# Row sums for the norms and the softmax as four 32-column tiles behind the rope matmuls, and another order of the first loads, in an 8-core hybrid attention block

## The chip, the cores and the metric

The kernel runs on the 8 cores of one Trainium2 chip. Each core computes one half of the positions of one of four batch entries (1024 of 2048), all heads, with no exchange between cores. The metric is the device time of the slowest core, in microseconds (us). Engines are named as in the profile: PE is TensorE (PEld its weight loads), ACT is ScalarE, DVE is VectorE, POOL is GpSimd, SP is SyncE, which only starts transfers here.

## What is computed

The reference, cut to what the change touches:

```python
h = rmsnorm(x, norm_g); z = h @ w_in            # split into latents, rope key, gates, conv inputs
q  = rmsnorm(q_a, q_lat_g) @ w_uq               # 16 heads x (128 + 64 rope)
kv = rmsnorm(kv_a, kv_lat_g) @ w_ukv            # 16 heads x (128 key + 128 value)
k  = concat(k_nope, k_pe for every head)
q, k = rmsnorm(q, q_norm_g), rmsnorm(k, k_norm_g)     # over the 192 columns of a head
q, k = rope on the last 64 columns
attn = softmax(q @ k.T * 192**-0.5) @ v               # all 2048 keys
y_attn = (attn * silu(gate_a)) @ w_branch_attn        # beside it a gated 3-tap convolution branch
x = x + merge(y_attn, y_conv) @ w_out                 # then a gated per-layer embedding is added
```

Activations lie with channels on partitions and positions in columns, so the sum of squares of a head's query or key, and the sum of a softmax, run over partitions. The kernel makes them on PE, with a matrix of ones as one operand.

## The kernel before

**Stages.** Opening: 16 tiles of x (513 KB each, six buffers) and 16 pieces of the latent weights (w_lq, w_lk; eight staging buffers) come in on SP's queue in a written order `seq`; ACT scales each x tile, DVE casts each weight piece, PE multiplies (`q_lat`, then `kv_own`). Then gate tiles and the other half's keys, to 240 us. From there the head loop runs to about 905 us; after it come the merge, the output projection and the embedding gate.

**The head loop.** For each head there are 16 key steps (kt 0 to 15, 128 keys each). In step kt the program emits for PE: `emit_nope` of the next step (two 512-column matmuls: scores), in odd steps `emit_rope` of the next two steps (four matmuls of 64 rows, which run two at a time), and `emit_PV` of this step (two 512-column matmuls). For ACT it emits `emit_exp` of the next step (128x1024). Score banks are 0 to 3, in two pairs by the step's parity.

Between these, one `quantum` of the convolution branch runs in each step (four matmuls of 512 columns, or five or six of 342). Where a quantum ends its PSUM bank (`ends_bank()`), it is emitted ahead of the scores (`early`), elsewhere behind them. The pattern repeats every two heads. In even heads the early steps are kt 2, 5, 8, 11 and 14, in odd heads kt 0, 4, 8, 12 and 15.

**Pieces.** During head h the queries, keys and values of head h+1 are made, in `up_pieces`: `kup` (keys, two matmuls; ACT copies the bank, then squares it), `qrope`, `qnope` (four matmuls; copy and square), `vup` (values; one copy), and the sums `qss` (query, three matmuls of 512 columns with `onesL`, `onesR`, `onesB`) and `kss` (key, 16 matmuls with one column each). `lsum` (softmax of the head before, fp32) is at kt 1. All pieces use one PSUM bank, bank 7 (`bU`): a piece can't begin until the one before it has been read out. `widen` spreads the factors of a sum over the partitions by four transfers on SP.

Engines take their instructions in the order in which the program emits them; an instruction that must wait holds those behind it. The pieces stand first in a step:

```python
fn, after = pieces.get(kt, (None, None))
if fn:
    fn(bU)
if kt == 1 and lsum:
    lsum(bU)
...
early = ends_bank()
```

Of the kernel before, what the change touches and what calls it, by code (L numbers as in the profile page):

```python
# [167 lines left out]
def build_nc():  # L168
# [12 lines left out]
    wlq_d = din("w_lq", [8, 128, 1024])  # L181
    wlk_d = din("w_lk", [8, 128, 768])
# [6 lines left out]
    with ExitStack() as es:  # L189
# [44 lines left out]
        onesL = small(BF16, 128, "onesL")  # L234
        onesR = small(BF16, 128, "onesR")
# [75 lines left out]
        def cast():
# [47 lines left out]
        for b_, boxes in ((onesL, ((0, 128, 0),)), (onesR, ((0, 128, 64),)), (onesB, ((0, 64, 0), (64, 128, 64)))):
            P.op("dve", lambda h, b_=b_: h.memset(b_.ap, 0.0), writes=[b_])  # L360
            for r0, r1, c0 in boxes:
                P.op("dve", lambda h, b_=b_, r0=r0, r1=r1, c0=c0: h.memset(b_.ap[r0:r1, c0:c0 + 64], 1.0), reads=[b_], writes=[b_])
# [645 lines left out]
        for h in range(NH):  # L1008
# [275 lines left out]
```

How the kernel before makes its waits and increments, by code:

```python
    def emit(self, eng, h, sems):  # L146
        waited = {}
        for o in self.ops[eng]:
            need = {}
            for d in o.deps:
                if d.slot is not None:
                    k, v, s = id(d.slot), d.val, d.slot.sem
                else:
                    if d.eng == "pe" and eng == "pe":
                        continue
                    k, v, s = d.eng, d.count, sems[d.eng]
                if waited.get(k, 0) < v and need.get(k, (0, None))[0] < v:
                    need[k] = (v, s)
            for k, (v, s) in need.items():
                h.wait_ge(s, v)
                waited[k] = v
            inst = o.fn(h)
            if o.slot is not None:
                inst.then_inc(o.slot.sem, 16)
            elif o.signal:
                inst.then_inc(sems[eng], 1)
```

## Time and profile before

| What | Value |
|---|---|
| Median of 3 runs | 1532.65 us (1531.38 to 1534.86) |
| The profiled execution | 1532.65 us, of which the span of core 6 is 1531.1 us |
| Spans of the 8 cores | 1523.3 to 1531.1 us |
| PE busy | 1496.2 us (98% of the span), 7854 matmuls |
| DVE, ACT, POOL busy | 839.5 us, 711.6 us, 224.0 us |
| Granted PE clock, mean by core | 0.997 to 1.000 |

The rows are of core 6, the slowest. A matmul's row has its start and a modelled duration, which holds some 0.16 us of pipeline behind the last column. Matmuls follow each other more closely than that, so the distance of two starts tells the cost, and a short wait of PE does not show as idle.

### The profile page before, as it was taken

The page shows a single profiled execution, that of the slowest core. Times are in us where ns is not written, and L with a number is a line of the kernel's source. Part 1 is how long each engine was busy: PE and PEld are TensorE (multiplying, and loading weights), DVE is VectorE, ACT ScalarE, POOL GpSimd, SP SyncE. Part 2 cuts the span into 40 slices and gives each one's busy share as a digit, 9 for nine tenths or more (in the row PEclk, how much of TensorE's full clock was granted, in tenths as well). Part 3 has the DMA queues.
Part 4 walks back from the last instruction along what each step waited for, and adds up shares of the span by engine and source line. Part 5 has one row for each costly group of instructions (what it writes and reads, how often), then busy time and mean ns, then how long its engine had stood idle before and what let it go on. Part 6 is the DMA issues. An engine that isn't in the chain of part 4 may idle for free.

```text
span 1531.1 us, 22610 instructions; the slowest of 8 cores (1523.3 to 1531.1 us)
## 1 busy us (share of the span) xinstructions
PE 1496.2 (98%) x7854; PEld 673.6 (44%) x7854; DVE 839.5 (55%) x1043; ACT 711.6 (46%) x966; POOL 224.0 (15%) x245
## 2 busy tenths in 40 slices
PE   6899999999999999999999999999999999999998
PEld 2344444444444444444444444444444444444443
DVE  5566565777766776766677762222222222444555
ACT  5565678777777777777776641100011100112111
POOL 0000000221303131222223121000010001000000
PEclk9999999999999999999999999999999999999999
DMA  8937542333333222333333217354453536984641
GB/s 271 265 71 178 122 83 58 72 57 72 72 71 60 54 59 58 72 70 72 69 59 63 56 35 124 56 90 70 75 91 55 97 60 139 219 174 76 135 117 73
DMA packets 52071, 144.15 MB, mean 94 GB/s; under 512 B 7668, under 2 KB 7670, under 8 KB 51832
## 3 DMA queue, kind: packets, MB, share of 16 engines
q0 software_dynamic: 23328, 78.13, 30.3%
q1 hardware_dynamic: 28480, 64.52, 14.3%
q8 instruction: 65, 1.06, 0.3%
q14 instruction: 46, 0.38, 0.1%
q10 hardware_dynamic: 152, 0.05, 0.0%
HBM read 188.81 MB, written 8.39 MB: 129 GB/s over the span
## 4 chain that ended last, share of the span: by engine, by line
PE 88%; DVE 3%; ACT 3%; issue 3%; DMA 2%; SPq 0%; DVEq 0%; ACTq 0%
PE ps L257 86%; PE ps L256 2%; DMA xo_89<-x_own 1%; DMA xo_88<-x_own 1%; DVE acc L271 1%; ACT eb_172 L260 0%; SPq L251 0%; ACT eb_173 L260 0%; ACT P_208 L260 0%; ACT P_210 L260 0%; ACT fall L260 0%; ACT P_209 L260 0%; DVE yb L263 0%; DVE Qn_204 L263 0%; ACT sqs_140 L260 0%
## 5 line engine op out<-in xcount | busy, mean ns | idle before, releaser
L271 DVE TENSOR_TENSOR acc<-acc,P_210 128x1024 f32<-128x1024 f32 x75 | 99.3, 1324 | 13.2 <-ACT P_210 L260 10.3
L271 DVE TENSOR_TENSOR acc<-acc,P_208 128x1024 f32<-128x1024 f32 x75 | 97.8, 1304 | 14.8 <-ACT P_208 L260 11.7
L271 DVE TENSOR_TENSOR acc<-acc,P_209 128x1024 f32<-128x1024 f32 x74 | 98.9, 1337 | 11.6 <-ACT P_209 L260 8.8
L257 PE MATMUL ps<-Qn_204,Kn_200 128*128 128x512 bf16 x256 | 76.6, 381 | 0.0
L257 PE MATMUL ps<-Qn_205,Kn_201 128*128 128x512 bf16 x256 | 76.2, 379 | 0.0
L260 ACT ACTIVATE mt_258<-mt_258 128x512 f32<-128x512 f32 x16 | 10.1, 632 | 123.6 <-DVE mt_258 L271 123.6
L260 ACT ACTIVATE mt_257<-mt_257 128x512 f32<-128x512 f32 x16 | 10.1, 632 | 120.0 <-DVE mt_257 L271 120.0
L251 POOL DMA_DIRECT2D ring_126<-w_tiles x23 | 12.9, 561 | 347.7 <-PE ps L257 283.6
L260 ACT ACTIVATE P_210<-ps,sk_54 128x1024 bf16<-128x1024 f32 x43 | 47.9, 1114 | 13.9 <-PE ps L257 7.4
L260 ACT ACTIVATE P_209<-ps,sk_55 128x1024 bf16<-128x1024 f32 x43 | 48.0, 1117 | 11.6 <-PE ps L257 10.8
L260 ACT ACTIVATE P_208<-ps,sk_54 128x1024 bf16<-128x1024 f32 x43 | 47.9, 1115 | 11.7 <-PE ps L257 7.2
L260 ACT ACTIVATE P_208<-ps,sk_55 128x1024 bf16<-128x1024 f32 x43 | 48.0, 1116 | 10.4 <-PE ps L257 9.8
L260 ACT ACTIVATE P_210<-ps,sk_55 128x1024 bf16<-128x1024 f32 x42 | 47.0, 1118 | 10.5 <-PE ps L257 8.0
L260 ACT ACTIVATE P_209<-ps,sk_54 128x1024 bf16<-128x1024 f32 x42 | 46.8, 1114 | 10.1 <-PE ps L257 5.5
L257 PE MATMUL ps<-Qr_206,KrT 64*128 64x512 bf16 x256 | 40.8, 385 | 1.9 <-ACT P_208 L260 0.7
L257 PE MATMUL ps<-Qr_207,KrT 64*128 64x512 bf16 x256 | 39.4, 381 | 0.8 <-ACT P_209 L260 0.3
L263 DVE SCALAR_TENSOR_TENSOR mt_262<-mt_258,ps 128x512 f32<-128x512 f32 x16 | 11.0, 688 | 44.0 <-PE ps L257 44.0
L274 POOL TENSOR_TENSOR zb<-zb,rst 128x512 f32<-128x512 f32 x16 | 31.8, 1990 | 22.2 <-ACT ebc L260 22.2
L271 DVE TENSOR_TENSOR mt_260<-ps,rst 128x512 f32<-128x512 f32 x16 | 11.1, 692 | 43.5 <-PE ps L257 43.5
L260 ACT ACTIVATE tp_308<-tp_306 128x512 f32<-128x512 f32 x16 | 10.1, 632 | 53.0 <-DVE tp_306 L271 53.0
L257 PEld LDWEIGHTS ps<-Qn_205,Kn_201 128*128 128x128 bf16 x256 | 22.4, 97 | 27.2 <-issue 9.4
L263 DVE SCALAR_TENSOR_TENSOR mt_261<-mt_257,ps 128x512 f32<-128x512 f32 x16 | 11.0, 688 | 41.8 <-PE ps L257 41.8
(1428 smaller groups left out, 4074.9 us busy)
## 6 DMA issues: line engine op xcount, KB each, us to landing
fb<-f_218 SPq DMA_DIRECT2D x128, 128.0 KB, 2.4
ring_127<-w_tiles POOLq DMA_DIRECT2D x28, 512.0 KB, 6.8
ring_129<-w_tiles POOLq DMA_DIRECT2D x28, 512.0 KB, 5.8
ring_126<-w_tiles POOLq DMA_DIRECT2D x23, 512.0 KB, 5.7
ring_128<-w_tiles POOLq DMA_DIRECT2D x22, 512.0 KB, 6.6
ringm_266<-w_tiles POOLq DMA_DIRECT2D x14, 512.0 KB, 6.3
ringm_265<-w_tiles POOLq DMA_DIRECT2D x9, 512.0 KB, 7.1
t_223<-q_221 SPq DMA_DIRECT2D x64, 64.0 KB, 2.0
```

What stands on the lines that cost most here:

```text
L251: return P.dma(eng, lambda h: h.dma_start(out=o_ap, in_=in_ap), slot, reads=reads, writes=[b], deps=deps)
L256: return P.op("pe", lambda h: h.matmul(bank_ap, lhsT=lhsT, rhs=rhs, start=start, stop=stop, skip_group_check=True), reads=reads, writes=wr ...
L257: return P.op("pe", lambda h: h.matmul(bank_ap, lhsT=lhsT, rhs=rhs, start=start, stop=stop), reads=reads, writes=writes)
L260: return P.op("act", lambda h: h.activation(out=out, in_=in_, func=func, **kw), reads=reads, writes=writes)
L263: return P.op("dve", lambda h: h.scalar_tensor_tensor(out=out, in0=in0, scalar=scalar, in1=in1, op0=op0, op1=op1), reads=reads, writes=writes)
L271: return P.op("dve", lambda h: h.tensor_tensor(out=out, in0=in0, in1=in1, op=op), reads=reads, writes=writes)
L274: return P.op("pool", lambda h: h.tensor_tensor(out=out, in0=in0, in1=in1, op=op), reads=reads, writes=writes)
```

## The change

It has three parts.

1. **The sums.** `qss` becomes eight matmuls, each 32 columns of the array wide with 256 moving columns; `kss` becomes four of 32 by 512, then a transpose on DVE; `lsum` becomes four of 32 by 256. Each of the four tiles writes another 32 partitions of bank 7. The two ACT instructions behind `qss` and `lsum` shrink from 512 to 256 columns. `widen` makes the same bytes in four transfers, each source row read four times. The query factors are applied in three places (kt 10, 12, 13) in place of one.
2. **The order in a step.** The pieces are emitted behind scores, exp and rope. `kup` 1 moves from kt 6 to kt 2, `qrope` from 2 to 3, `qnope` from 4 and 5 to 5 and 6.
3. **The opening.** Three small loads (positions, `sel`, `cols`) go ahead of all else on SP in place of ACT's queue; w0 is requested before x0; there are four staging buffers in place of eight; w_lq and w_lk lie in another layout, each load still 4 KB or 3 KB per partition.

```diff
-        stage = [at((RING0 if i < 4 else W0 + 45408) + i % 4 * 4096, F32, 1024, f"stage{i}") for i in range(8)]
+        stage = [at(W0 + 45408 + i * 4096, F32, 1024, f"stage{i}") for i in range(4)]
...
-        seq = ("x0 w0 x1 w1 x2 x3 w2 x4 x5 w3 x6 x7 w4 x8 x9 w5 x10 x11 w6 w7 x12 w8 w9 x13 w10 w11 x14 w12 w13 x15 w14 w15").split()
+        seq = ("w0 x0 x1 w1 x2 x3 w2 x4 x5 w3 x6 x7 w4 x8 x9 w5 x10 x11 w6 w7 x12 w8 w9 x13 w10 w11 x14 w12 w13 x15 w14 w15").split()
...
-                    if int(n[1:]) - 8 >= cast_n[0]:
+                    if int(n[1:]) - 4 >= cast_n[0]:
...
+        ld("sp", posi, pos_d, out_ap=posi.ap[0:2, :])
+        ld("sp", sel, sel_d, out_ap=sel.ap[0:2, :])
+        ld("sp", cols, cols_d)
         issue()
-        ld("act", posi, pos_d, out_ap=posi.ap[0:2, :])
-        ld("act", sel, sel_d, out_ap=sel.ap[0:2, :])
-        ld("act", cols, cols_d)
...
+        def quarters(q):
+
+            return q // 2, slice((q % 2) * 256, (q % 2) * 256 + 256), slice(q * 32, q * 32 + 32)
+
         def widen(src):
 
-            for qb in range(2):
-                for r in range(2):
-                    ld("sp", fb, src.ap[qb * 64:qb * 64 + 64, :], out_ap=fb.ap[r * 64:r * 64 + 64, qb * 512:(qb + 1) * 512], reads=[src])
+            (pitch, _), (_, n) = src.ap.ap
+            for q in range(4):
+                rows = bass.AP(src.ap.tensor, src.ap.offset + q * 32 * pitch, [[pitch, 32], [0, 4], [1, n]])
+                ld("sp", fb, rows, out_ap=fb.ap[:, q * n:(q + 1) * n], reads=[src])
...
             def qss(bk):
-                for i, l_ in enumerate((onesL, onesR, onesB)):
-                    mm(bk.ap, l_.ap, qsq[i].ap, i == 0, i == 2, [l_, qsq[i]], [bk])
-                act(f2.ap, bk.ap, AF.Ln, [bk, cols], [f2], bias=col(C_EPS), scale=1.0 / 192)
+                for part in range(2):
+                    for q in range(4):
+                        hf, n, r = quarters(q)
+                        l_ = onesB.ap[:, hf * 64:hf * 64 + 32] if part else ones.ap[:, 0:32]
+                        s_ = qsq[2] if part else qsq[hf]
+                        mm(bk.ap[r, 0:256], l_, s_.ap[:, n], part == 0, part == 1, [onesB, ones, s_], [bk], skip=True)
+                act(f2.ap, bk.ap[:, 0:256], AF.Ln, [bk, cols], [f2], bias=col(C_EPS), scale=1.0 / 192)
...
             def kss(bk):
-                for j in range(16):
-                    s_ = ksq[j // 4]
-                    mm(bk.ap[:, j:j + 1], s_.ap[:, (j % 4) * 128:(j % 4 + 1) * 128], ones.ap[:, 0:1], j == 0, j == 15, [s_, ones], [bk], skip=True)
-                tt(skt[p].ap, bk.ap[:, 0:16], sspe.ap, ADD, [bk, sspe], [skt[p]])
+                kv_ = ksqa.ap.rearrange("p (t q n) -> p q t n", q=4, n=32)
+                for q in range(4):
+                    mm(bk.ap[q * 32:q * 32 + 32, :], ones.ap[:, 0:32], kv_[:, q], True, True, [*ksq, ones], [bk], skip=True)
+                tr = t12[1]
+                P.op("dve", lambda h: h.transpose(out=tr.ap, in_=bk.ap), reads=[bk], writes=[tr])
+                tt(skt[p].ap, tr.ap[:, 0:512:32], sspe.ap, ADD, [tr, sspe], [skt[p]])
...
-            return {0: (pc(kup, 0), None), 2: (pc(qrope), qrope_out), 4: (pc(qnope, 0), None), 5: (pc(qnope, 1), lambda bk: rot()), 6: (pc(kup, 1), None), 7: (pc(qss), None),
-                    8: (pc(kup, 2), None), 9: (pc(kup, 3), None), 10: (pc(vup, 0), lambda bk: qfin()), 11: (pc(kss), None), 12: (pc(vup, 1), None), 13: (pc(vup, 2), None),
-                    14: (pc(vup, 3), None)}
+            return {0: (pc(kup, 0), None), 2: (pc(kup, 1), None), 3: (pc(qrope), qrope_out), 5: (pc(qnope, 0), None), 6: (pc(qnope, 1), lambda bk: rot()), 7: (pc(qss), None),
+                    8: (pc(kup, 2), None), 9: (pc(kup, 3), None), 10: (pc(vup, 0), lambda bk: qn_out(0)), 11: (pc(kss), None), 12: (pc(vup, 1), lambda bk: qn_out(1)),
+                    13: (pc(vup, 2), lambda bk: qr_out()), 14: (pc(vup, 3), None)}
...
             def lsum(bk):
-                for qb in range(2):
-                    r = slice(qb * 64, qb * 64 + 64)
-                    mm(bk.ap[r, :], onesf.ap[:, r], acc.ap[:, qb * 512:(qb + 1) * 512], True, True, [onesf, acc], [bk], twin=qb == 1)
-                act(f2.ap, bk.ap, AF.Ln, [bk], [f2], scale=2.0)
+                for q in range(4):
+                    mm(bk.ap[q * 32:q * 32 + 32, 0:256], onesf.ap[:, 0:32], acc.ap[:, q * 256:(q + 1) * 256], True, True, [onesf, acc], [bk], skip=True)
+                act(f2.ap, bk.ap[:, 0:256], AF.Ln, [bk], [f2], scale=2.0)
...
-                if fn:
-                    fn(bU)
-                if kt == 1 and lsum:
-                    lsum(bU)
                 if kt == 15:
...
                     emit_exp(g + 1)
                     if first:
                         emit_rope(g + 2, True)
+                if fn:
+                    fn(bU)
+                if kt == 1 and lsum:
+                    lsum(bU)
```

**PE's order in steps kt 8 and 9 of an odd head.** Step 8 is an early one. `kvaT` rows are a `kup` piece, `xh` rows the convolution quantum, `Qn` rows the scores, `Qr` rows rope, `P` rows PV. Before:

```order
L257 MATMUL ps<-kvaT_145,wup_187 128x512 [waits s_act]
L257 MATMUL ps<-kvaT_146,wup_187 128x512
L257 MATMUL ps<-xh_68,ring_129 128x512
L257 MATMUL ps<-xh_69,ring_129 128x512
L257 MATMUL ps<-xh_70,ring_129 128x512
L257 MATMUL ps<-xh_71,ring_129 128x512
L257 MATMUL ps<-Qn_205,Kn_201 128x512 x2
L257 MATMUL ps<-P_208,V_203 128x512 [waits s_act]
L257 MATMUL ps<-P_208,V_203 128x512
L257 MATMUL ps<-kvaT_145,wup_187 128x512 [waits s_act]
L257 MATMUL ps<-kvaT_146,wup_187 128x512
L257 MATMUL ps<-Qn_205,Kn_201 128x512 x2
```

The same place in the change, from the last matmul of the quantum:

```order
L255 MATMUL ps<-xh_69,ring_123 128x512
L255 MATMUL ps<-Qn_199,Kn_195 128x512 x2
L255 MATMUL ps<-kvaT_139,wup_181 128x512 [waits s_act]
L255 MATMUL ps<-kvaT_140,wup_181 128x512
L255 MATMUL ps<-P_202,V_197 128x512 x2
L255 MATMUL ps<-Qn_199,Kn_195 128x512 x2
L255 MATMUL ps<-Qr_201,KrT 128x512 x2
L255 MATMUL ps<-Qr_201,KrT 128x512 [waits s_act]
L255 MATMUL ps<-Qr_201,KrT 128x512
L255 MATMUL ps<-kvaT_139,wup_181 128x512 [waits s_act]
L255 MATMUL ps<-kvaT_140,wup_181 128x512
```

Between the two pieces there stood the quantum, one pair of scores and PV. Now there stand PV, one pair of scores and a block of rope.

**PE's order around the query sum, kt 7 of an odd head.** `qsq` rows are `qss`. Before:

```order
L257 MATMUL ps<-P_209,V_203 128x512
L257 MATMUL ps<-qsq_215,onesL 128x512 [waits s_act]
L257 MATMUL ps<-qsq_216,onesR 128x512
L257 MATMUL ps<-qsq_217,onesB 128x512
L257 MATMUL ps<-Qn_205,Kn_201 128x512 x2
L257 MATMUL ps<-Qr_207,KrT 128x512 x2
```

Now:

```order
L255 MATMUL ps<-Qn_199,Kn_195 128x512 x2
L255 MATMUL ps<-Qr_201,KrT 128x512 x2
L255 MATMUL ps<-Qr_201,KrT 128x512 [waits s_act]
L255 MATMUL ps<-Qr_201,KrT 128x512
L254 MATMUL ps<-qsq_206,ones 32x256 [waits s_act]
L254 MATMUL ps<-qsq_206,ones 32x256
L254 MATMUL ps<-qsq_207,ones 32x256 x2
L254 MATMUL ps<-qsq_208,onesB 32x256 x4
```

The three full matmuls ahead of the scores have become eight small ones directly behind rope.

## Rows read from the trace of the kernel before

**Rows 1.** Windows: window, length, busy us (and instructions) of each engine, clock, DMA.
```profile
0.00:50.00 50.00, 31.04 (x103) 11.03 (x103) 28.48 (x44) 31.08 (x33) 0.20 (x4) 0.97 0.85 277
240.00:905.00 665.00, 661.39 (x4015) 297.72 (x4014) 469.87 (x513) 476.92 (x649) 159.14 (x123) 1.00 0.31 62
```

**Rows 2.** Timeline of PE: softmax sum, scores, rope; start, duration, instruction.
```profile
449.70 1.08 PE L257 MATMUL ps<-acc,onesf 128*64 128x512 f32 x4
450.71 0.61 PE L257 MATMUL ps<-Qn_205,Kn_201 128*128 128x512 bf16 x2
451.25 0.60 PE L257 MATMUL ps<-Qr_207,KrT 64*128 64x512 bf16 x4
451.78 0.39 PE L257 MATMUL ps<-xh_56,ring_128 128*128 128x512 bf16 x1
```

**Rows 3.** Timeline of PE: `qrope`, `qss` and `kss`, with what follows them.
```profile
453.18 0.41 PE L257 MATMUL ps<-qaT_72,wup_187 128*64 128x512 bf16 x2
453.42 0.38 PE L257 MATMUL ps<-qaT_73,wup_187 128*64 128x512 bf16 x2
...
466.26 0.38 PE L257 MATMUL ps<-qsq_215,onesL 128*128 128x512 bf16 x1
...
466.91 0.59 PE L257 MATMUL ps<-Qn_205,Kn_201 128*128 128x512 bf16 x2
...
476.41 0.24 PE L256 MATMUL ps<-ones,ksq_211 128*128 128x1 bf16 x4
...
476.81 0.59 PE L257 MATMUL ps<-Qn_205,Kn_201 128*128 128x512 bf16 x2
```

**Rows 4.** Timeline, kt 8 to 9 of an odd head; brackets: idle time, releaser.
```profile
470.57 0.59 PE L257 MATMUL ps<-Qn_205,Kn_201 128*128 128x512 bf16 x2
...
471.32 1.11 ACT L260 ACTIVATE P_210<-ps,sk_55 128x1024 bf16<-128x1024 f32 x1 [0.27 <-PE ps L257]
...
472.33 0.58 ACT L918 CAST Kn_200<-ps 128x512 bf16<-128x512 f32 x1
...
472.80 0.61 ACT L260 ACTIVATE ksq_214<-ps 128x512 bf16<-128x512 f32 x1
```

**Rows 5.** Timeline, kt 2 to 3 of an even head.
```profile
413.77 0.59 PE L257 MATMUL ps<-Qn_204,Kn_200 128*128 128x512 bf16 x2
...
414.52 1.11 ACT L260 ACTIVATE P_209<-ps,sk_54 128x1024 bf16<-128x1024 f32 x1 [0.86 <-PE ps L257]
...
415.17 0.39 PE L257 MATMUL ps<-Qr_206,KrT 64*128 64x512 bf16 x2
...
415.78 0.39 PE L257 MATMUL ps<-Qr_206,KrT 64*128 64x512 bf16 x2 [0.23 <-ACT P_209 L260]
```

**Rows 6.** Timeline, kt 11 to 12 of an odd head.
```profile
478.75 0.59 PE L257 MATMUL ps<-P_209,V_203 128*128 128x512 bf16 x2
479.17 0.17 DVE L271 TENSOR_TENSOR skt_52<-ps,sspe 128x16 f32<-128x16 f32 x1
...
479.48 0.22 PE L256 MATMUL ps<-wup_187,kvaT_145 128*128 128x128 bf16 x1
```

**Rows 7.** The costliest groups: instruction, count | busy us, mean ns | idle before.
```profile
L271 DVE TENSOR_TENSOR mt_260<-ps,rst 128x512 f32<-128x512 f32 x16 | 11.1, 692 | 43.5 <-PE ps L257 43.5
```

**Rows 8.** Timeline: SP's four transfers of one `widen`, and their first user.
```profile
468.86 2.43 SPq L251 DMA_DIRECT2D fb<-f_218  x4
...
477.66 0.73 DVE L263 SCALAR_TENSOR_TENSOR Qn_204<-q_220,colx,fb 128x512 bf16<-128x512 f32 x1
```

**Rows 9.** Timeline of the opening (SPq and ACTq are transfer requests).
```profile
1.07 0.54 ACTq L251 DMA_DIRECT2D posi<-pos_row  x1
...
1.91 0.37 ACTq L251 DMA_DIRECT2D cols<-cols  x1
...
11.36 1.15 ACT L260 ACTIVATE xh_56<-xo_84,cols 128x1026 bf16<-128x1026 f32 x1 [7.49 <-DMA cols<-cols]
...
44.36 1.15 ACT L260 ACTIVATE xh_67<-xo_89,cols 128x1026 bf16<-128x1026 f32 x1 [1.61 <-DMA xo_89<-x_own]
...
48.52 0.38 PE L257 MATMUL ps<-xh_56,wlk_116 128*128 128x512 bf16 x1 [0.97 <-ACT qraw_82 L421]
```

More of the change, by code:

```diff
@@ L180, in build_nc @@
     sel_d = din("sel", [2, 128])
-    wlq_d = din("w_lq", [8, 128, 1024])
-    wlk_d = din("w_lk", [8, 128, 768])
+    wlq_d = din("w_lq", [128, 16, 512])
+    wlk_d = din("w_lk", [128, 16, 384])
     wup_d = din("w_up", [NH, 128, 1280])
@@ L233, in build_nc @@
         onesf = small(F32, 128, "onesf")
-        onesL = small(BF16, 128, "onesL")
-        onesR = small(BF16, 128, "onesR")
         onesB = small(BF16, 128, "onesB")
@@ L304, in ld_part @@
             kind, i = order[n]
-            b = stage[n % 8]
+            b = stage[n % 4]
             if kind == "q":
-                ld("sp", b, wlq_d[i])
+                ld("sp", b, wlq_d[:, i * 2:(i + 1) * 2, :], out_ap=b.ap.rearrange("p (c n) -> p c n", c=2))
             else:
-                ld("sp", b, wlk_d[i], out_ap=b.ap[:, 0:768])
+                ld("sp", b, wlk_d[:, i * 2:(i + 1) * 2, :], out_ap=b.ap[:, 0:768].rearrange("p (c n) -> p c n", c=2))
         def cast():
@@ L314, in cast @@
             kind, i = order[n]
-            b = stage[n % 8]
+            b = stage[n % 4]
             if kind == "q":
@@ L349, in casts_to @@
                     issue()
+        ld("sp", posi, pos_d, out_ap=posi.ap[0:2, :])
+        ld("sp", sel, sel_d, out_ap=sel.ap[0:2, :])
+        ld("sp", cols, cols_d)
         issue()
-        ld("act", posi, pos_d, out_ap=posi.ap[0:2, :])
-        ld("act", sel, sel_d, out_ap=sel.ap[0:2, :])
-        ld("act", cols, cols_d)
         P.op("dve", lambda h: h.memset(ones.ap, 1.0), writes=[ones])
-        act(sspe.ap[:, 0:1], ones.ap[:, 0:1], AF.Copy, [ones], [sspe])
         P.op("dve", lambda h: h.memset(onesf.ap, 1.0), writes=[onesf])
[L359 to L362, printed above, removed]
+        P.op("dve", lambda h: h.memset(onesB.ap, 0.0), writes=[onesB])
+        for r in (0, 64):
+            P.op("dve", lambda h, r=r: h.memset(onesB.ap[r:r + 64, r:r + 64], 1.0), reads=[onesB], writes=[onesB])
         vcopy(posf.ap[0:2, :], posi.ap[0:2, :], [posi], [posf])
@@ L397, in q_lat @@
                 mm(banks[i].ap, w_.ap[:, o + m * 128:o + (m + 1) * 128], xh[kc].ap[:, qb * 512:(qb + 1) * 512], kc == first, kc == last, [w_, xh[kc]], [banks[i]])
+        act(colx.ap[:, 3:4], ones.ap[:, 0:1], AF.Copy, [ones], [colx])
+        casts_to("x0")
         kv_next = 0
@@ L837, in build_nc @@
         Pt = [take(BF16, T, f"P{i}") for i in range(3)]
-        ksq = [take(BF16, 512, f"ksq{i}") for i in range(4)]
+        ksqa = take(BF16, S, "ksqa")
+        ksq = [Buf(ksqa.ap[:, i * 512:(i + 1) * 512], f"ksq{i}") for i in range(4)]
+        for b in ksq:
+            b.alias = ksqa.alias
         qsq = [take(BF16, 512, f"qsq{i}") for i in range(3)]
-        f2 = take(F32, 512, "f2")
+        f2 = take(F32, 256, "f2")
         fb = take(F32, T, "fb")
@@ L1200, in part @@
         return np.ascontiguousarray(w.reshape(k // 128, 128, n).transpose(1, 0, 2))
-    def pairs(w):
-        k, n = w.shape
-        return np.ascontiguousarray(w.reshape(k // 256, 2, 128, n).transpose(0, 2, 1, 3).reshape(k // 256, 128, 2 * n))
     conv = np.stack([tiles(w_in[:, c:c + 1024]) for c in (C_CC, C_CX, C_GC, C_CB)], axis=1).reshape(32, 128, 2048)
@@ L1246, in _host_inputs @@
         "sel": ((np.arange(128) // 32 % 2)[None, :] == np.arange(2)[:, None]).astype(f32),
-        "w_lq": pairs(w_in[:, 0:512]),
-        "w_lk": pairs(np.concatenate([w_in[:, 512:768], kpe, kpe[:, perm]], axis=1)),
+        "w_lq": part(w_in[:, 0:512]),
+        "w_lk": part(np.concatenate([w_in[:, 512:768], kpe, kpe[:, perm]], axis=1)),
         "w_up": np.ascontiguousarray(wup),
```

13 lines of the change are left out of this document (6 added, 7 removed).

## The prediction

> **What bounds the kernel now.** I read the windows first. From 240 to 905 us, the head loop in which the change lies, PE is busy 661 of 665 us at the full clock, while DVE has 470 and ACT 477 [rows 1]. So a column taken from PE there is time, and so is each wait added to it; work added to DVE or ACT costs nothing until PE waits for it. Then I read PE's timeline, by the distance of starts. Three matmuls of 512 columns take 0.65 us [rows 3], so one is 0.217 and a pair 0.43. The scores at 450.71 should be through at 451.14, but rope starts at 451.25; rope's four matmuls, two at a time, should be through at 451.68, and the next full matmul starts at 451.78 [rows 2]. Each change between the full array and a tiled one thus costs 0.10 to 0.11 us, and a block of rope 0.11 + 0.43 + 0.10 = 0.64. Last I looked for places where PE waits. There are two kinds, and both matter below.
>
> The first kind stands after an early step that has no piece behind its scores. The scores start at 413.77, the exp on them at 414.52, and it ends at 415.63. The second half of rope, which overwrites the bank that this exp reads, was ready 0.22 behind 415.17, at 415.39, and starts at 415.78, 0.15 after the exp's end: PE lost 0.39 [rows 5]. This stands once in each of the eight even heads 0 to 14. The second kind is at `vup` in the seven odd heads 1 to 13: PV should be through at 479.18, DVE frees bank 7 at 479.34, `vup` starts at 479.48, 0.30 late [rows 6].
>
> **What the sums save on PE.** `qrope` shows two tiles of 64 columns at once: a pair of them is 0.22 to 0.24, like one full matmul [rows 3]. I take it that four tiles of 32 do the same.
> - `qss`: 0.65 [rows 3] becomes two rounds of 256 columns, 0.22. It also lies between two tiled shapes, and no row shows whether PE pays for going from one to the other: 0 or 0.11. I take the nearest row, 0.10 [rows 2]. Saved: 0.33.
> - `kss`: 16 matmuls take 0.40 [rows 3]; one round of 512 columns and the 0.10 take 0.32. Saved: 0.08.
> - `lsum`: 1.01 from its start to the scores, 0.16 of it beyond its column time of 0.85 [rows 2], and 0.10 ahead of it: 1.11. Now half the columns, 0.43, and the 0.16: 0.59. Saved: 0.52.
> - `qrope` behind rope spares one change of shape: 0.10.
>
> That is 1.03 us a head, 15.5 for the 15 heads with pieces. Outside the loop the first head's `qss` gives 0.23 and the last `lsum` 0.43. In all 16.2 us.
>
> On tile-to-tile changes the Trainium skill (TensorEngine Tiling (Array Packing), Key Properties) says that changing the tiling mode, and not only the tile, drains the engine; no run here shows that step yet. By it the 0.10 above would stay.
>
> **What the order costs.** Bank 7 is one, and a piece waits until ACT has read the one before. Before, a piece stood first in its step, ACT read it at once, and the quantum, scores and PV lay between it and the next piece. Now ACT first gets the exp of the same step, since that is emitted ahead of the piece. Rows 4 give ACT's chain at just such a place: scores start at 470.57, exp at 471.32, copy at 472.33, square at 472.80, ending at 473.41; with the 0.15 of rows 5 the bank is free 2.99 us after the scores began [rows 4, 5]. In a step that is not early the quantum, up to four times 0.217 us, lies behind the piece as well, and this fits. In an early step the quantum lies ahead of the scores, so that PE comes to the next piece after scores 0.43, `kup` 0.43, PV 0.43, scores 0.43 and rope 0.64 = 2.36 us [rows 2, 3]. It waits 0.63.
> - Four places are of this kind: even heads kt 2 to `qrope` and kt 8 to `kup` 3; odd heads kt 0 to `lsum` and kt 8 to `kup` 3.
> - Even heads, `qnope` 0 (kt 5) to `qnope` 1: the exp, 0.32 (that is 0.75 less 0.43) behind its first pair of rope [rows 4], starts as `qnope` does; the copy waits for `qnope`'s end, 0.86 + 0.32 = 1.18, the square starts 0.47 later and ends at 2.26, the bank is free at 2.41. PE is back after 0.86 + 0.43 + 0.43 = 1.72. It waits 0.69.
> - Odd heads, kt 4 is early and has no piece any more: the wait of rows 5, 0.39.
> - `vup` 2 behind early `vup` 1 in odd heads: 0.75 + 1.01 + 0.58 + 0.15 = 2.49 against 2.37 (`vup` has eight matmuls of 128 columns where `kup` has two of 512), 0.12 [rows 4].
> - Even heads, `kss` (kt 11) to `vup` 1: bank 7 is freed by the transpose. No row shows one; the bounds are the 0.17 of a small DVE instruction [rows 6] and twice the 0.692 of one that reads 128x512 from PSUM [rows 7]. I take 0.69, the row nearest in shape. The sum's 0.22, the 0.32 to the next engine, 0.69 and 0.15 make 1.38 against 0.32 + 0.43 + 0.43 = 1.18, but part of the sum's drain lies under the wait: about 0.1 lost. With the lower bound nothing is lost, with the upper 0.7 more, 6 us over eight heads.
>
> Even heads lose 0.63 + 0.63 + 0.69 + 0.1 = 2.05, eight of them 16.4; odd heads 0.63 + 0.63 + 0.39 + 0.12 = 1.77, seven of them 12.4: 28.8 us. In return the waits of today go. In even heads `kup` now stands in kt 2 behind the scores and gives the exp 0.43 more: 8 x 0.39 = 3.1. In odd heads DVE has one query product ahead of `kss` in place of three, and PE comes later: 7 x 0.30 = 2.1 [rows 5, 6]. Together 5.2.
>
> **What costs nothing.** DVE gets the transpose and one product more, some 1.4 us a head, in a loop in which it is idle for 195 us [rows 1]; without that room it would cost 21 us. ACT's logarithms and exponentials on half the columns are off PE's path. The four transfers of `widen` have rows half as long; their requests end at 471.29 and the first user starts at 477.66 [rows 8], so even twice the request time, 2.43 us more, is hidden; if it were not, DVE would reach `kss` late, at the price of the upper bound above.
>
> **The opening.** Transfers are busy 0.85 of the first 50 us, at 277 GB/s [rows 1], and ACT waits for the twelfth x tile until 44.36, behind which PE's dense key matmuls start at 48.52 [rows 9]. The first big request is now made behind three small ones, whose requests take from 1.07 to 2.28 [rows 9]: 1.2 us later, and the same bytes stand ahead of the twelfth tile. So +1.2. From below: today the first tile waits for `cols` until 11.36 [rows 9], and the change has both by about 9 us (1 MB at 277 GB/s behind the requests); if the stream is not what holds, 2.4 us are gained. From above, four staging buffers for eight may leave the stream dry behind the casts; I allow as much again, +2.4. `xo_89` is ahead of all loads that wait so.
>
> **The sum** is made against the profiled execution, 1532.65 us with a span of 1531.1, which is also the median: 1532.65 - 16.2 - 5.2 + 28.8 + 1.2 = 1541.3, about 1541.
>
> **Rivals.**
> - *ACT is done in time* (faster). If the chain from scores to free bank fell from 2.99 below 2.36 us, the waits would vanish and the savings stay: 1541 less 28.8 is 1512. For it: ACT is idle a quarter of the loop. Against it: rows 5, where PE waits for the exp alone. Chance 0.12.
> - *Half of the waits.* PE's lost time in one place lets ACT and DVE run ahead, and later waits shrink: 1527 to 1535. Chance 0.13.
> - *The tiles do not run side by side.* Then qss takes 0.86, kss 0.86, lsum 1.71 of column time in place of 0.22, 0.22 and 0.43: 2.56 a head, 38 us, 1579. Rows 3 speak against it with two tiles. Chance 0.04.
> - *They run side by side, but start late.* If a round of four took a quarter longer than one tile, 0.22 a head, it would be 1544. The Trainium skill (TensorE: Matmul & The Clock Gate, Part 3) has three 32-column tiles at 2.38 times one; an estimate by that share is 0.23 a head, 1545. Chance 0.05.
> - *The transpose is twice the price*: 1547. Chance 0.06.
> - *The opening is not held by the stream*: 1541 - 1.2 - 2.4 = 1537. Chance 0.05.
>
> **How the numbers follow.** The forecast has 0.55. A measurement of this kernel can tell about 0.2%, 3 us: 1529.6 to 1535.7 is no change. Faster: the first rival and a third of the second, 0.16. The same: the rest of the second and the lower edge of the forecast, 0.09 + 0.07 = 0.16. Slower: 0.68. The range of 1527 to 1551 leaves out the first rival and the third, and a few hundredths at the edges; its ends are half the waits gone below, and the transpose's and the opening's upper bounds, 1541 + 6 + 1.2 with some late tiles, above. The forecast's own range is 1535 to 1547.
>
> **What would show it.** In the changed kernel's timeline `qss`, `kss` and `lsum` should take 0.2 to 0.6 us from their start to the next start, and lie directly behind rope. `qrope` and `kup` 3 of even heads and `lsum` and `kup` 3 of odd heads should start about 0.15 behind the end of ACT's square, some 0.6 late. An even and an odd head together should take 1.1 us more than now (3.82 of waits come, 0.69 go, 2.06 are saved). Wrong it would be if those pieces start without a gap, if rows of ACT show the copy ahead of the exp, or if PE's dense key matmuls start well before 48.

## The result and the profile after

| | Before | The change |
|---|---|---|
| Median | 1532.1 us | 1543.1 us |
| Ratio to before, 95% interval | | 1.0067 [1.0047, 1.0087] |
| Slowest span of the profiled execution | 1531.1 us (core 6) | 1541.8 us (core 1) |

Medians, here and in the table of the runs, are of the executions in which no half of the cores ran at a lowered clock; some expectations quote medians of all executions, up to 0.4 us higher.

The change is slower by 0.67%. The prediction had 1541, with slower as the likeliest sign. The loss is not made up as the prediction has it, though: the head loop is nearly as forecast, the opening has the other sign, and a loss of six to seven microseconds ahead of the loop was not seen.

First the window of the head loop in the changed kernel, with the columns of [rows 1]:

```profile
240.00:905.00 665.00, 641.25 (x3934) 292.02 (x3935) 487.18 (x540) 460.33 (x649) 147.10 (x119) 1.00 0.32 62
```

In the head loop PE is busy 641 us in place of 661. The columns are saved, but no time is gained: the 20 us are now idle, and the loop is longer. The timeline shows where. First two places where nothing waits: `lsum` in an even head, then `qss` and `kss`, each with the rope ahead and the row behind.

```profile
330.20 0.61 PE L255 MATMUL ps<-Qr_200,KrT 64*128 64x512 bf16 x4
...
330.74 0.64 PE L254 MATMUL ps<-acc,onesf 128*32 128x256 f32 x8
...
331.31 0.32 PE L255 MATMUL ps<-xh_59,ring_120 128*128 128x342 bf16 x1
...
346.91 0.61 PE L255 MATMUL ps<-Qr_200,KrT 64*128 64x512 bf16 x4
...
347.45 0.29 PE L254 MATMUL ps<-qsq_206,ones 128*32 128x256 bf16 x2
...
347.78 0.32 PE L255 MATMUL ps<-xh_59,ring_120 128*128 128x342 bf16 x1
...
358.37 0.40 PE L254 MATMUL ps<-ksqa,ones 128*32 128x512 bf16 x4
...
358.70 0.60 PE L255 MATMUL ps<-P_203,V_196 128*128 128x512 bf16 x2
358.89 0.72 DVE L936 STREAM_TRANSPOSE t_214<-ps 128x512 f32<-128x512 f32 x1 [0.80 <-PE ps L254]
```

From start to next start `lsum` takes 0.57, `qss` 0.33 and `kss` 0.33, where they took 1.01, 0.65 and 0.40 [rows 2, 3]. Four matmuls of 512 columns in 0.33, of which 0.22 is the time of one and 0.11 the change of shape: the four tiles run side by side. From rope's start to `lsum` there are 0.54, 0.43 of columns and 0.11: going from one tiled shape to another costs the same 0.11 as going to the full array does at these places.

Now step kt 8 to 9 of an even head, which answers to [rows 4], and `lsum` in an odd head:

```profile
349.83 0.59 PE L255 MATMUL ps<-Qn_198,Kn_194 128*128 128x512 bf16 x2
...
350.57 1.11 ACT L258 ACTIVATE P_204<-ps,sk_52 128x1024 bf16<-128x1024 f32 x1 [1.04 <-PE ps L255]
...
351.59 0.58 ACT L928 CAST Kn_195<-ps 128x512 bf16<-128x512 f32 x1
...
351.65 0.60 PE L255 MATMUL ps<-Qr_200,KrT 64*128 64x512 bf16 x4
...
352.05 0.61 ACT L258 ACTIVATE ksqa<-ps 128x512 bf16<-128x512 f32 x1
...
352.81 0.38 PE L255 MATMUL ps<-kvaT_139,wup_182 128*128 128x512 bf16 x1 [0.55 <-ACT ksqa L258]
...
371.96 0.60 PE L255 MATMUL ps<-Qr_201,KrT 64*128 64x512 bf16 x4
...
373.12 0.64 PE L254 MATMUL ps<-acc,onesf 128*32 128x256 f32 x8 [0.55 <-ACT ksqa L258]
```

Scores at 349.83, bank free for `kup` 3 at 352.81: 2.98 us. PE was ready at 351.65 + 0.43 + 0.10 = 352.18 and lost 0.63. `lsum` lost the same behind `kup` 0. The row names the square that PE waited for.

From the softmax sum in head 2 to that in head 14 there are six pairs of heads. They began at 324.90 and 826.93 before. Now the first is at 330.74 (above), and the last is

```profile
838.57 0.64 PE L254 MATMUL ps<-acc,onesf 128*32 128x256 f32 x8
```

A pair took 502.03 / 6 = 83.67 us and takes 507.83 / 6 = 84.64, 0.97 more. This measure serves for every run below.

Three rows of the slowest core of each profile divide the rest of the time: the sum of squares of x behind the opening, the first scores, the last softmax sum. Before:

```profile
70.31 1.03 PE L257 MATMUL ps<-accx,onesf 128*128 128x342 f32 x3
...
237.92 1.06 PE L257 MATMUL ps<-Qn_204,Kn_200 128*128 128x512 bf16 x2
...
904.40 1.08 PE L257 MATMUL ps<-acc,onesf 128*64 128x512 f32 x4
```

Now:

```profile
67.66 1.31 PE L255 MATMUL ps<-accx,onesf 128*128 128x342 f32 x4
...
241.37 1.06 PE L255 MATMUL ps<-Qn_198,Kn_194 128*128 128x512 bf16 x2
...
915.46 0.64 PE L254 MATMUL ps<-acc,onesf 128*32 128x256 f32 x8
```

The opening ends 2.65 us earlier, the stretch to the first scores is 6.1 longer (173.71 for 167.61), the loop 7.6 longer (674.09 for 666.48). With -0.4 behind the loop that is the 10.7 us between the spans. The 6.1 is in the first head's pieces, which are made ahead of the loop in the order of the same table:

```profile
219.94 2.40 SPq L249 DMA_DIRECT2D t_214<-q_212  x4
...
221.38 0.53 POOL L249 DMA_DIRECT2D ring_122<-w_tiles  x1 [9.20 <-PE ps L255]
...
226.95 0.59 ACT L884 COPY q_212<-ps 128x512 f32<-128x512 f32 x1 [3.16 <-DMA t_214<-q_212]
...
227.44 0.60 ACT L258 ACTIVATE qsq_207<-ps 128x512 bf16<-128x512 f32 x1
...
228.18 0.40 PE L254 MATMUL ps<-qsq_207,ones 128*32 128x256 bf16 x2 [4.11 <-ACT qsq_207 L258]
...
228.73 0.61 PE L255 MATMUL ps<-xh_64,ring_123 128*128 128x512 bf16 x1
...
233.40 0.57 PE L255 MATMUL ps<-xh_57,ring_123 128*128 128x512 bf16 x1
```

`qss` stands still for 4.11 us. It waits for the second square, this for the copy into `q0[1]` ahead of it on ACT, and this for the four transfers that swap halves for rope: `q0[1]` is also their source. The fourth of them, requested 0.4 us behind the 512 KB load on POOL, lands 5.1 us after its request; before, that load was requested 3.5 us behind the first transfer in place of 1.4, and all four landed in 2.0. Behind the stall the eleven matmuls from 228.73 to 233.40 stand 0.42 apart in place of 0.22, which is 1.2 GHz in place of 2.4; they cost 2.3 us more. Stall and clock make 6.4, and the rest of the stretch is 0.3 shorter than before. All 8 cores have this stall, of 4.0 to 5.2 us.

### The profile page after: what moved, and what is told of

Same layout as the page of the kernel before. It is cut to its first block, busy times and chain, and to the rows that moved or that the text cites. A ratio compares the mean times of both kernels' runs of the same rounds, so it can differ in the third digit from the quotient of the medians.

```text
span 1541.8 us, 22482 instructions; the slowest of 8 cores (1536.5 to 1541.8 us)
## 1 busy us (share of the span) xinstructions
PE 1485.9 (96%) x7806; PEld 671.5 (44%) x7806; DVE 862.9 (56%) x1071; ACT 695.9 (45%) x966; POOL 217.5 (14%) x245
## 4 chain that ended last, share of the span: by engine, by line
PE 85%; ACT 7%; issue 4%; DMA 2%; DVE 2%; SPq 0%; ACTq 0%; DVEq 0%
PE ps L255 81%; PE ps L254 3%; ACT ksqa L258 1%; DMA stage_95<-w_lk 1%; DMA xo_83<-x_own 1%; ACT P_202 L258 1%; ACT P_204 L258 1%; ACT P_203 L258 1%; ACT Kn_195 L928 1%; ACT Kn_194 L928 1%; ACT eb_166 L258 0%; DMA t_214<-q_212 0%; ACT q_211 L884 0%; ACT qsq_206 L258 0%; ACT fall L258 0%
## 5 line engine op out<-in xcount | busy, mean ns | idle before, releaser
L269 DVE TENSOR_TENSOR acc<-acc,P_202 128x1024 f32<-128x1024 f32 x75 | 103.5, 1380 | 7.7 <-ACT P_202 L258 3.6
L269 DVE TENSOR_TENSOR acc<-acc,P_204 128x1024 f32<-128x1024 f32 x75 | 101.9, 1359 | 6.4 <-DVE acc L269 3.1
L269 DVE TENSOR_TENSOR acc<-acc,P_203 128x1024 f32<-128x1024 f32 x74 | 99.0, 1338 | 6.7 <-ACT P_203 L258 3.1
L258 ACT ACTIVATE mt_249<-mt_249 128x512 f32<-128x512 f32 x16 | 10.1, 630 | 123.3 <-DVE mt_249 L269 123.3
L258 ACT ACTIVATE mt_248<-mt_248 128x512 f32<-128x512 f32 x16 | 10.1, 630 | 120.1 <-DVE mt_248 L269 120.1
L258 ACT ACTIVATE ksqa<-ps 128x512 bf16<-128x512 f32 x64 | 39.2, 612 | 0.0
L255 PEld LDWEIGHTS ps<-Qn_199,Kn_195 128*128 128x128 bf16 x256 | 24.9, 97 | 27.9
L255 PEld LDWEIGHTS ps<-Qn_198,Kn_194 128*128 128x128 bf16 x256 | 24.9, 98 | 24.3 <-issue 0.8
```

What stands on the lines that cost most here:

```text
L255: return P.op("pe", lambda h: h.matmul(bank_ap, lhsT=lhsT, rhs=rhs, start=start, stop=stop), reads=reads, writes=writes)
L258: return P.op("act", lambda h: h.activation(out=out, in_=in_, func=func, **kw), reads=reads, writes=writes)
L269: return P.op("dve", lambda h: h.tensor_tensor(out=out, in0=in0, in1=in1, op=op), reads=reads, writes=writes)
```

## The experiments

The theory after the trace: three losses and gains that add up, the place within a step (slower, by waits for bank 7), the order of the first head's pieces (slower), the tiles (faster); and the opening with little effect. Ratios are to the kernel before on the same chip, measured beside the run. Runs 1 to 4, 5 to 8, 9 and 10, and 11 were measured together; the kernel before took 1532.1 to 1534.9 us in these sessions and the first one. So a difference of less than 3 us between runs of different sessions is uncertain, unless the time of a pair shows it.

| Run | Median, us | Ratio [95%] | A pair of heads, us |
|---|---|---|---|
| The change | 1543.1 | 1.0067 [1.0047, 1.0087] | 84.64 |
| 1 Pieces ahead of the scores | 1522.2 | 0.9911 [0.9872, 0.9950] | 81.81 |
| 2 Ahead in early steps alone | 1538.8 | 1.0032 [1.0001, 1.0063] | 83.99 |
| 3 First head's order mended | 1536.4 | 1.0012 [0.9989, 1.0034] | 84.63 |
| 4 Before, with the new opening | 1530.4 | 0.9968 [0.9947, 0.9990] | 83.68 |
| 5 Edits 1 and 3 together | 1516.8 | 0.9883 [0.9865, 0.9902] | 81.81 |
| 6 Squares from the copies | 1526.8 | 0.9952 [0.9936, 0.9968] | 82.36 |
| 7 Another source of the swap | 1538.9 | 1.0033 [1.0018, 1.0047] | 84.60 |
| 8 Before, with the new place alone | 1546.8 | 1.0080 [1.0065, 1.0096] | 85.32 |
| 9 As 5, sums behind rope where free | 1515.1 | 0.9878 [0.9859, 0.9897] | 81.65 |
| 10 As 5, pieces at the old steps | 1519.7 | 0.9906 [0.9890, 0.9923] | 82.18 |
| 11 Weight load behind the swap | 1539.7 | 1.0030 [1.0004, 1.0056] | 84.57 |

**1. Pieces ahead of the scores.**

```diff
                 fn, after = pieces.get(kt, (None, None))
+                if fn:
+                    fn(bU)
+                if kt == 1 and lsum:
+                    lsum(bU)
...
                     if first:
                         emit_rope(g + 2, True)
-                if fn:
-                    fn(bU)
-                if kt == 1 and lsum:
-                    lsum(bU)
```

> The change with its pieces, sums included, put back ahead of the scores in every step; the four array tiles, the new places in the head, the opening and the first head's order stay as in the change. Theory (new waits of 0.63 us on bank 7 come from pieces that stand behind the rope matmuls of an early step, with nothing but one step's scores between them): those 28.8 us go, the drains that the place behind rope saved come back (about 0.4 us a head, 6 us), and the 5.2 us of old waits come back at most: 1543.2 - 28.8 + 6 + (0 to 5.2) = 1520 to 1526 us. Rival (the loop is longer because of the narrow tiles themselves, not their place): no more than a third of it goes, 1533 to 1545 us.

Measured 1522.2, 20.9 us below the change, and a pair takes 2.83 less. The place of the pieces is the loss, not the tiles. The same two `kup` pieces, of an odd head, in this run:

```profile
387.04 0.59 PE L255 MATMUL ps<-kvaT,wup 128*128 128x512 bf16 x2
...
387.73 0.58 ACT L928 CAST Kn<-ps 128x512 bf16<-128x512 f32 x1 [0.43 <-PE ps L255]
...
388.21 0.60 ACT L258 ACTIVATE ksqa<-ps 128x512 bf16<-128x512 f32 x1
...
388.77 0.59 PE L255 MATMUL ps<-P,V 128*128 128x512 bf16 x2
...
389.08 1.11 ACT L258 ACTIVATE P<-ps,sk 128x1024 bf16<-128x1024 f32 x1 [0.27 <-PE ps L255]
389.20 0.59 PE L255 MATMUL ps<-kvaT,wup 128*128 128x512 bf16 x2
```

Copy and square now come ahead of the exp on ACT, the bank is free at 388.8, and the next `kup` starts at 389.20 directly behind PV.

**2. Ahead in early steps alone.** In early steps the two pieces' lines are emitted ahead of the quantum, in the others behind rope.

```diff
                 early = ends_bank()
                 if early:
+                    emit_piece()
                     quantum()
...
-                if fn:
-                    fn(bU)
-                if kt == 1 and lsum:
-                    lsum(bU)
+                if not early:
+                    emit_piece()
```

> The change with the pieces put ahead of the scores in early steps alone (those in which the fill-in matmuls also stand ahead of the scores); in the other steps they stay behind the rope matmuls. Theory: a piece in an early step is now followed by fill-in matmuls and two groups of scores' worth of time before bank 7 is wanted again, so the 0.63 and 0.69 us rows vanish; drains come back in the few early steps only (under 2 us): 1543.2 - 28.8 + 2 = about 1516 us, at most 1521 with the old waits. Rival (the wait moves to the piece before, since from a step that is not early to an early one only one set of fill-in matmuls now lies between): half of the waits stay, about 1530 us.

Measured 1538.8: the theory's 1516 failed, and the rival was right that the wait moves, if not on where or how much. The rows at 0.63 are gone, and this stands at six places of a pair:

```profile
309.58 2.33 ACT L258 ACTIVATE P<-ps,sk 128x1024 bf16<-128x1024 f32 x2 [0.27 <-PE ps L255]
309.70 0.59 PE L255 MATMUL ps<-Qn,Kn 128*128 128x512 bf16 x2
...
310.23 0.39 PE L255 MATMUL ps<-Qr,KrT 64*128 64x512 bf16 x2
...
310.84 0.39 PE L255 MATMUL ps<-Qr,KrT 64*128 64x512 bf16 x2 [0.23 <-ACT P L258]
```

The second half of rope waits 0.39 for the exp, as in [rows 5]. In a step behind an early one, scores and rope alone are too short for the exp on ACT; a piece ahead of the scores there is what covers it. So whichever comes behind the rope of such a step is late: the bank, or the rope itself.

**3. First head's order mended.**

```diff
-        for i, (fn, after) in enumerate(up_pieces(0).values()):
+        first_up = up_pieces(0)
+        for i, (fn, after) in enumerate(first_up[k] for k in (0, 3, 5, 6, 2, 7, 8, 9, 10, 11, 12, 13, 14)):
```

> The change with the second key piece of the first head put back between its last query piece and its query sums, ahead of the loop; all else as in the change. Theory (the query sums of the first head wait 4.1 us for a copy that waits for the swap transfers, and the clock falls to half behind that): the stall shrinks to 2 us or less and the clock stays up, 4 to 6 us less than the change, 1537 to 1539 us. Rival (the transfers themselves are later, whatever follows them): the stall only moves to the next piece, 1542 to 1544 us.

Measured 1536.4, 6.8 below the change, with the pair unchanged at 84.63. The four transfers land in 2.0 us again, and `qss` does not wait. The window of its slowest core shows the clock up, 1.00 in the first row (this run) against 0.80 in the second (the change); the third row is of before:

```profile
220.00:245.00 25.00, 21.64 (x139) 10.17 (x137) 12.35 (x18) 19.83 (x36) 1.58 (x3) 1.00 0.47 88
```
```profile
220.00:245.00 25.00, 19.08 (x102) 8.35 (x101) 9.13 (x15) 14.87 (x27) 1.58 (x3) 0.80 0.44 82
```
```profile
220.00:245.00 25.00, 22.97 (x144) 11.12 (x144) 10.28 (x16) 20.42 (x35) 1.59 (x3) 0.93 0.48 88
```

So the clock fell there before the change too, on five of the 8 cores and for 3.4 us; in run 3 it does so on one core.

**4. Before, with the new opening.** Only the hunks of the opening (SP's order, four staging buffers, layout; also the places of ACT's first copy and of the first cast).

```diff
-                    if int(n[1:]) - 8 >= cast_n[0]:
+                    if int(n[1:]) - 4 >= cast_n[0]:
...
+        ld("sp", posi, pos_d, out_ap=posi.ap[0:2, :])
+        ld("sp", sel, sel_d, out_ap=sel.ap[0:2, :])
+        ld("sp", cols, cols_d)
         issue()
```

> The kernel before with the change's opening alone (small loads first on SP, four staging buffers, the other layout of the weights, first weight ahead of the first x tile); the head loop as before. Theory (the slowest core's start of the first key matmuls varies by core more than it moved): no change within 0.15 percent, 1530.5 to 1534.5 us. Rival of the prediction on record: plus 1.2 us, 1533.3 us. Rival from the two profiled cores, whose openings differ by 2.65 us: 1529.5 us.

Measured 0.9968, a gain of 1.5 to 8 us: neither the no-change that the theory had nor the predicted loss, and nearest to the second rival, though not for its reason. The start of the sum of squares on all 8 cores tells more than that of one. With the old opening it spreads from 62.60 to 70.31 (before) and from 62.48 to 70.34 (run 8), with the new one from 65.28 to 68.91 (the change). In the eleven profiles with the new opening the latest core is at 67.19 to 69.45, 68.6 in the mean. So the latest core comes 1.7 us earlier, and the mean of the cores does not (66.3 before, 66.9 in the change). The slowest core is the metric. There are only two profiles with the old opening; whether the gain is more than these 1.7 us is open.

**5. Edits 1 and 3 together.**

> The change with its pieces ahead of the scores in every step and with the first head's second key piece back between its last query piece and its query sums. Theory (two separate losses: place behind the rope matmuls, measured at 20.7 us by the first of these edits, and order of the first head's pieces, measured at 6.8 us by the second): both come off, 1543.2 - 20.7 - 6.8 = 1515.7 us, between 1513.5 and 1518. Rival (the first head's stall had been there partly because of the clock, and what remains is hidden by the loop's opening): 1519 to 1522.6 us.

Measured 1516.8: the two add up, 26.4 us against 27.7.

**6. Squares from the copies.**

```diff
-                act(qsq[qb].ap, bk.ap, AF.Square, [bk], [qsq[qb]])
+                act(qsq[qb].ap, q0[qb].ap, AF.Square, [q0[qb]], [qsq[qb]])
...
-                act(ksq[tb].ap, bk.ap, AF.Square, [bk], [ksq[tb]])
+                act(ksq[tb].ap, K_.ap[:, sl], AF.Square, [K_], [ksq[tb]])
```

> The change with one thing altered: the squares of the key and query pieces are taken from the copies in SBUF in place of bank 7, so that the bank is free 0.47 to 0.60 us earlier (after ScalarE's copy alone); ScalarE's work and its order stay, and the key's squares are of the rounded copy. Theory (the waits behind the rope matmuls are for bank 7, which the square holds): the five rows of 0.63 and 0.69 us in a pair of heads fall by some 0.48 each, 2.4 us a pair over 7.5 pairs = 18 us: 1525 us. Rival (what runs last is ScalarE's whole chain, so that the wait shows again at the next rope matmul, 0.39 us at a place, as it did when the pieces of early steps were put ahead): half of it, 1532 to 1536 us. Rival (the bank is not what they wait for): 1543 us.

Measured 1526.8, 16.3 below the change; a pair takes 2.28 less where 2.4 was expected. At the place of `kup` 3 in an even head:

```profile
348.44 0.58 ACT L928 CAST Kn<-ps 128x512 bf16<-128x512 f32 x1
348.51 0.60 PE L255 MATMUL ps<-Qr,KrT 64*128 64x512 bf16 x4
...
349.11 0.63 ACT L258 ACTIVATE ksqa<-Kn 128x512 bf16<-128x512 bf16 x1
...
349.17 0.59 PE L255 MATMUL ps<-kvaT,wup 128*128 128x512 bf16 x2
```

`kup` 3 starts 0.66 behind rope's start in place of 1.16, and 0.15 behind the end of the copy, while the square has just begun. ACT does the same work in the same order; what was taken away is the square's hold on the bank. This is the direct proof that the waits are for bank 7.

**7. Another source of the swap.**

```diff
-                src = q0[1]
+                src = q0[1] if h else Osb
```

> The change with another buffer as the source of the first head's four swap transfers (one that nothing uses yet), so that the copy of the second query piece does not wait for them; the order of the pieces stays as in the change. Theory (that copy is what the query sums wait for, 4.1 us, and the transfers end late because a 512 KB weight load runs beside them): the stall goes with the wait, 6 to 7 us less than the change, 1536 to 1537 us. Rival (the missing key piece is what counts, since without it the sums stand directly behind their own squares): 1 to 2 us of stall and the low clock stay, 1539 to 1541 us.

Measured 1538.9, near the rival's 1539 to 1541: 4.2 us of the 6.8 that run 3 gives. The copy no longer waits, and the longest wait of the query sums is 0.85 us. The transfers still land late (6.2 us), and later pieces now wait: `kss` 2.10 us for its squares, where it waits 0.83 in run 3. The clock over 220 to 245 us is 0.93, as before. So the wait of the copy is not all: without the second key piece between query piece and query sums some 2.5 us are missing, an amount that differences between sessions could blur.

**8. Before, with the new place alone.** The diff of run 1 the other way round, on the kernel before.

> The kernel before with its old sums, its own order of pieces in a head and its opening, and only the place within a step altered: pieces behind the rope matmuls. Theory (the place alone makes the waits, whatever the sums are): new waits at five places in a pair of heads (query piece to key piece and key piece to key piece in the even head; sums of the softmax behind the first key piece, query piece to query piece and key piece to key piece in the odd one), 3.3 us, less 0.7 us of old waits and 0.2 to 0.4 us of drains: 2.3 to 2.6 us a pair over 7.5 pairs, 17 to 20 us: 1550 to 1554 us. Rival (the waits need the new sums, whose transpose holds the bank): within 3 us of before, 1530 to 1536 us.

Measured 1546.8, less than the 1550 to 1554 expected, but slower than the whole change. A pair takes 1.65 more than before: by the distances of starts the five new waits are three of 0.63, one of 0.68 and one of 0.20, 2.8 in place of 3.3. With the change's sums and steps the same move costs 2.8 a pair (run 5 to run 3); there `qrope` and rope itself wait too. The waits are there without tiles or transposes: `kup` 3 of an even head starts at 438.02 behind rope at 436.86, the same 1.16 apart as in the change.

**9. As 5, sums behind rope where the bank has long been free.**

```diff
+                behind = kt in (1, 3, 7, 11) and not early and not was_early
+                was_early = early
...
+                if not behind:
+                    emit_piece()
...
+                if behind:
+                    emit_piece()
```

> As the run with both edits undone (pieces ahead of the scores, first head's order mended; 1516.8 us), but the query rope piece and the three sums stand behind the rope matmuls in those steps where neither their own step nor the step ahead is an early one: five places in a pair of heads (query sums in both heads, softmax sums in the even head, query rope piece and key sums in the odd one). Theory (the place behind the rope matmuls costs nothing where bank 7 has long been free, and saves a drain of 0.10 us, up to 0.2 with the half-array tile): 0.5 to 1.0 us a pair over 8 pairs, 4 to 8 us less, 1509 to 1513 us. Rival (a piece behind the rope matmuls always makes something late, by ScalarE's order): 0.4 us at three or more of the five places, 1516 to 1522 us.

Measured 1515.1, and a pair takes 0.16 less than in run 5: right in sign, about a quarter of the size, and by the runs alone not to be told from run 5 (the intervals overlap). Where PE has less to do ahead of rope, rope itself waits for the exp again: at `qss` of an even head its four matmuls take 0.88 in place of 0.61.

```profile
416.74 1.12 ACT L258 ACTIVATE P<-ps,sk 128x1024 bf16<-128x1024 f32 x1
...
417.52 0.88 PE L255 MATMUL ps<-Qr,KrT 64*128 64x512 bf16 x4
...
418.32 0.29 PE L254 MATMUL ps<-qsq,ones 128*32 128x256 bf16 x4
```

**10. As 5, pieces at the old steps.** The table of `up_pieces` has the keys of the kernel before (`qrope` 2, `qnope` 4 and 5, `kup` 1 at 6).

> As the run with both edits undone (1516.8 us), but with the pieces of a head at the steps of the kernel before (query rope piece at step 2, second key piece at step 6), so that against the kernel before with the new opening (1530.7 us) only the four array tiles, the transposed key sums and the outputs in three parts differ. Theory (of the 13.9 us between these two, 4 to 5 are old waits that the new places in the head removed, and 9 to 10 are the tiles' columns): 1520 to 1522 us. Rival (the tiles bring all of it): 1516 to 1518 us.

Measured 1519.7. From run 4 to here, tiles, transpose and the split of the query products: 10.7 us, 1.50 a pair. From here to run 5, the new steps: 2.9 us, 0.37 a pair. Of the two old waits the rows of this run have one, rope in an even head, and not the other, `vup` in an odd head, which now stands directly behind PV:

```profile
328.72 0.39 PE L255 MATMUL ps<-Qr,KrT 64*128 64x512 bf16 x2
329.34 0.39 PE L255 MATMUL ps<-Qr,KrT 64*128 64x512 bf16 x2 [0.23 <-ACT P L258]
...
391.25 0.18 DVE L269 TENSOR_TENSOR skt<-t,sspe 128x16 f32<-128x16 f32 x1
...
391.52 0.59 PE L255 MATMUL ps<-P,V 128*128 128x512 bf16 x2
...
391.95 0.61 PE L254 MATMUL ps<-wup,kvaT 128*128 128x128 bf16 x8
```

**11. Weight load behind the swap.**

```diff
                     o = ld("sp", t12[1], src.ap[r * 32:r * 32 + 32, :], out_ap=t12[1].ap[d_ * 32:d_ * 32 + 32, :], reads=[src])
+                    if h == 0:
+                        swaps.append(o)
...
-                    ld("pool", b, src, out_ap=b.ap[:, 0:n], deps=deps)
+                    ld("pool", b, src, out_ap=b.ap[:, 0:n], deps=[*deps, *swaps])
+                    swaps.clear()
```

> The change with one wait added on POOL: the weight load that is requested next after the first head's four swap transfers (512 KB) is requested only when those have landed. Theory (the swap transfers, which elsewhere land 2.0 us after their request, take 5.1 in the first head because that load runs beside them): they land in 2.0 to 2.6 us, the copy of the second query piece comes 2.5 to 3 us earlier, and the wait of the query sums shrinks from 4.1 to 1 to 1.6 us; the load itself comes some 3 us later with slack. 1538 to 1541 us. Rival (the transfers are slow for their place in the queue, or of themselves): landing and wait as in the change, 1542 to 1545 us.

Measured 1539.7. The first head's transfers now land in 2.0 us, the slowest on any core in 2.04, and the query sums wait 1.03 in place of 4.11:

```profile
224.07 0.59 ACT L886 COPY q<-ps 128x512 f32<-128x512 f32 x1
...
224.58 0.53 POOL L249 DMA_DIRECT2D ring<-w_tiles  x1 [12.20 <-PE ps L254]
...
225.30 0.29 PE L254 MATMUL ps<-qsq,ones 128*32 128x256 bf16 x2 [1.03 <-ACT qsq L258]
```

The load beside the transfers is what makes them late. They are half of the loss: 3.4 of the 6.8 us are gained, and the sums still stand directly behind their own squares.

## Why the prediction was right, and where it was not

**The sums: right.** The column times (0.43, 0.22 and 0.22 with 0.11 to 0.14 behind them) are those predicted. Without the place behind rope the prediction's own terms are `qss` 0.23, `kss` -0.02 and `lsum` 0.42 a head, 1.26 a pair; with the wait of `vup` that goes with the split products, 0.30, that is 1.56, and run 10 against run 4 measures 1.50. The rivals of tiles one after the other, or late to start, are out. An estimate by the Trainium skill (TensorE: Matmul & The Clock Gate, Part 3) put the late start at 0.23 a head; the rows show none. The trace agrees with the rule of the Trainium skill that a change of tiling mode drains the engine (TensorEngine Tiling (Array Packing), Key Properties), from one tiled shape to another too: 0.11 us from rope to `qss`.

**The waits: right, place by place.** Beyond the drain the rows show 0.63 at all four places of that kind, 0.63 for `qnope` 1 (0.69 predicted), 0.39 in rope, 0.06 at `vup` 2 (0.12) and 0.18 at `vup` 1 (0.1), 3.78 a pair. One wait more, 0.25 a pair, was not forecast: PV of an even head's first step stands until DVE has read what PV of the head before left in its bank. The transpose took 0.716 us in the median, where 0.69 was chosen; its rival is out. In a pair the prediction had +1.1, the trace has +0.97. As steps: from run 5 to run 3, where the place alone changes, 2.82 a pair, against 3.78 of waits less some 0.8 of drains that the place spares, 3.0. Runs 1, 6 and 8 show the cause from three sides. The first rival (ACT in time) and the second (half of the waits) are out.

**The old waits: right.** The term was 0.39 a pair in rope and 0.30 at `vup`. The first goes from run 10 to run 5, where a pair gains 0.37. The second goes from run 4 to run 10, with the split of the query products.

**The opening: wrong.** The step that failed is "1.2 us later, and the same bytes stand ahead of the twelfth tile. So +1.2." It was worked out from one core's profile. The cores start this stage up to 8 us apart, and the new order draws them together: the latest is 1.7 us earlier. The prediction's own sign of being wrong came: the dense key matmuls of the profiled core start at 44.11. The rival of an opening not held by the stream had the sign of this, but not the reason: the first tile is scaled at 10.3 to 11.7 us on the 8 cores, not at 9 (7.8 to 11.4 before). Which of its edits draws the cores together was not tried.

**The first head: missed.** The failed step is that outside the loop "the first head's `qss` gives 0.23". The prediction followed the table's new keys in the loop alone. Ahead of the loop the same table is walked without steps, so that moving `kup` 1 from key 6 to key 2 puts `qss` directly behind `qnope` 1, and the swap transfers one piece later, into the next weight load. This costs 6.8 us by run 3 (5.5 between runs 1 and 5).

So 1541 is near 1543 in part by luck: a loss of 6 to 7 us that was missed is set against an opening forecast 3 us too late and a loop forecast 0.5 us too long.

**The better version.** Tiles, new steps and opening, with the pieces ahead of the scores and the first head's old order, take 1516.8 us, 1.17% [0.98, 1.35] less than before; the sums behind rope where the bank is free bring 1.7 more by the medians, which the intervals do not tell from nothing.

## What to carry to other kernels

A piece of work that shares one PSUM bank with the next is not done when PE is done with it, but when its reader is; before moving it, follow the reader's own queue, since an instruction put ahead of the read there counts too. To give the bank back sooner (taking the second use from the copy) brought back 16 of the 21 us that the move had cost. And a table that sets an order may be walked in more than one place: each has its own cover for the same stall.

## What was not expected of the hardware

The swap transfers of 64 KB each (32 partitions of 512 fp32) land 2.0 us after their request in the median. In the first head of the change's profile the fourth, requested 0.4 us behind a 512 KB load on another queue, lands 5.1 us after its request, 0.2 us behind that load; over the 8 cores it is 5.0 to 6.2 us. When the load waits (run 11), all four land in 2.0. A single stall of PE of 4.1 us was followed by a stretch at 1.2 GHz: the granted clock from 220 to 245 us was 0.80, and 1.00 in run 3, where the stall was gone. The stall is not the only cause of such a fall: the window has 0.93 before the change, without it.
